# Head sums of a linear-attention trunk as two rounded products, at later places of the plan

## The reference

```python
def gla_out(o, r, norm_w):
    o = o * lax.rsqrt(jnp.mean(o * o, axis=-1, keepdims=True) + EPS) * norm_w.astype(jnp.float32)
    bsz, h, n, dv = o.shape
    o = o.transpose(0, 2, 1, 3).reshape(bsz, n, h * dv)
    return (o * jax.nn.silu(r.astype(jnp.float32))).astype(r.dtype)
```

## Time and profile before

| | |
|---|---|
| median of 3 runs | 1081.17 us (1080.87 to 1081.6) |
| the profiled execution | 1081.7 us |
| its span, first to last instruction | 1079.9 us |
| PE busy | 1055.8 us, 98% |
| DVE busy | 825.2 us, 76% |
| ACT busy | 510.8 us, 47% |
| POOL busy | 307.3 us, 28% |
| mean granted clock of PE | 0.997 |

### The profile page before, as it was taken

How to read it: one execution, slowest core, us unless ns; L and a number is a source line. 1 busy time by engine, 2 the same in 40 slices (tenths; PEclk the granted TensorE clock), 3 DMA queues, 4 the chain that set the end, 5 groups by cost and what they waited for, 6 DMA issues and landing times.

```text
span 1079.9 us, 16429 instructions
## 1 busy us (share of the span) xinstructions
PE 1055.8 (98%) x5576; PEld 852.4 (79%) x5576; DVE 825.2 (76%) x1062; ACT 510.8 (47%) x827; POOL 307.3 (28%) x280
## 2 busy tenths in 40 slices
PE   8999999999999999999999999999999999999996
PEld 5678888777778888887888888888778888888884
DVE  4878868647455986899887787877987777787776
ACT  5666533456525222677766666676422222222234
POOL 1000006486101443012332323233322222222323
PEclk9999999999999999999999999999999999999998
DMA  9633331101013664226866666768745844864604
GB/s 352 247 98 118 117 117 40 40 22 40 21 56 120 253 221 169 78 98 234 316 246 260 227 273 233 257 248 298 296 167 234 350 193 178 329 267 179 254 1 156
DMA packets 66646, 199.82 MB, mean 185 GB/s; under 512 B 5664, under 2 KB 15136, under 8 KB 66592
## 3 DMA queue, kind: packets, MB, share of 16 engines
q1 hardware_dynamic: 66592, 199.11, 49.2%
HBM read 139.32 MB, written 59.77 MB: 184 GB/s over the span
## 4 chain that ended last, share of the span: by engine, by line
PE 49%; DVE 5%; issue 1%; DVEq 0%; ACT 0%
PE main L1453 13%; PE ob L1411 13%; PE sm L1411 10%; PE sm L1453 8%; PE ob L1453 6%; DVE stage L2562 1%; DVE XR L2681 1%; DVE XR L2748 1%; DVE slot L2507 1%; DVE slot L2512 1%; DVE stage_last L2562 0%; DVE t_tmp L2555 0%; DVE hid L2569 0%; DVE t_tmp L2546 0%; DVE t_tmp L2541 0%
## 5 line engine op out<-in xcount | busy, mean ns | idle before, releaser
L958 PE MATMUL main<-a_hi,w_hi 128*128 128x512 f32 x376 | 125.9, 416 | 0.0
L1411 PE MATMUL ob<-h_sum,slot 128*128 128x512 f32 x504 | 121.2, 389 | 2.2 <-DVE hid L2569 2.1
L1882 ACT ACTIVATE slot<-raw 128x512 fp32r<-128x512 f32 x80 | 50.2, 631 | 153.1 <-PE main L1453 58.4
L958 PE MATMUL main<-a_lo,w_hi 128*128 128x512 f32 x376 | 116.5, 391 | 0.0
L958 PE MATMUL main<-a_hi,w_lo 128*128 128x512 f32 x376 | 116.2, 390 | 0.0
L1411 PEld LDWEIGHTS ob<-h_sum,slot 128*128 128x128 f32 x504 | 94.5, 188 | 22.5 <-issue 2.5
L2681 DVE SCALAR_TENSOR_TENSOR XR<-main,small,XR 128x512 f32<-128x512 f32 x112 | 83.3, 748 | 28.8 <-PE main L1453 27.7
L958 PEld LDWEIGHTS main<-a_lo,w_hi 128*128 128x128 f32 x376 | 70.6, 188 | 15.6
L958 PEld LDWEIGHTS main<-a_hi,w_lo 128*128 128x128 f32 x376 | 70.6, 188 | 15.5
L958 PEld LDWEIGHTS main<-a_hi,w_hi 128*128 128x128 f32 x376 | 66.7, 188 | 18.0 <-issue 5.8
L1453 PE MATMUL main<-t_even,slot 128*128 128x512 f32 x336 | 78.1, 389 | 0.0
(11 more groups left out here) (338 smaller groups left out, 2448.3 us busy)
## 6 DMA issues: line engine op xcount, KB each, us to landing
hidden_kept<-stage SPq DMA_DIRECT2D x98, 512.0 KB, 4.3
raw<-wstream SPq DMA_DIRECT2D x60, 512.0 KB, 4.2
t_even<-hidden_kept SPq DMA_DIRECT2D x56, 512.0 KB, 5.4
raw<-wstream SPq DMA_DIRECT2D x16, 1024.0 KB, 5.5
stage<-hidden_kept SPq DMA_DIRECT2D x21, 512.0 KB, 5.1
stage_last<-hidden_kept SPq DMA_DIRECT2D x21, 512.0 KB, 5.9
wmod<-wm SPq DMA_DIRECT2D x8, 1024.0 KB, 10.5
mbuf<-wm SPq DMA_DIRECT2D x16, 512.0 KB, 4.0
```

Source lines behind the costliest of these rows:

```text
L958: ins = pe.matmul(main[:, bank, half * HALF:(half + 1) * HALF], w[:, slot, k, :], x[:, half * HALF:(half + 1) * HALF], start=begin, stop=end)
L1411: ins = pe.matmul(hid_bank(acc, odd), slots1[j][:, w, kp, :], parts[x][:, kp, :], start=PARTS[j][3] and kp == 0 and m == 0, stop=kp == KP ...
L1882: act.activation(slots2[j][:, 0, :, :, :], operand(s, j), ACT.Copy).then_inc(w2_hi, 1)
```

## The change

Each head's squares are split into a rounded part (sqo_hi, made by a copy on ACT) and a low part (sqo_lo, made by a subtraction on DVE in a new job "sl"). Each head sum becomes two rounded products with a rounded matrix of ones (ones_r, made once) that are added up in the bank. The sums move to later places: from 4 and 5 places behind the first O of their head to 6 and 7 (heads 0 and 2) or 8 and 9 (heads 1 and 3). The first group's pooling products move from 10.6 and 10.7 to 10.4 and 10.5, and the decay of head 3's states from 14.1 and 14.2 to 14.4 and 14.5. The new buffers take the places of old ones: sqo_lo overwrites sqo, and sqo_hi lies where rso does.

```diff
-MIX_AT = (9 * 8, 11 * 8 + 6, 13 * 8 + 2, 14 * 8 + 1)
+MIX_AT = (9 * 8, 11 * 8 + 6, 13 * 8 + 2, 14 * 8 + 4)
+SPLIT_AT = (4, 4, 3, 4)
+SUMS_AT = (6, 8, 6, 8)
...
-    put_all(OUT_AT[_h] + 4, 1, ("ns", _h, 0), ("ns", _h, 1))
+    put_all(OUT_AT[_h] + SPLIT_AT[_h], 1, ("sl", _h))
+    put_all(OUT_AT[_h] + SUMS_AT[_h], 1, ("ns", _h, 0), ("ns", _h, 1))
...
-    put(10, 6 + _i, "pl", 0, _i)
+    put(10, 4 + _i, "pl", 0, _i)
...
+        sqo_lo = at("sqo_lo", [P, N], F32R, ZF + 10 * KIB)
+        sqo_hi = at("sqo_hi", [P, N], F32R, ZF + 14 * KIB)
...
             def head_sums(h, i):
                 b = begin_small(("ns", h, i))
-                pe.wait_ge(sqo_made, h + 1)
-                pe.matmul(sm[:, b, :], ones, sqo[:, i * HALF:(i + 1) * HALF], start=True, stop=True).then_inc(small_done, 1)
+                pe.wait_ge(sqo_split, h + 1)
+                cols = slice(i * HALF, (i + 1) * HALF)
+                pe.matmul(sm[:, b, :], ones_r[:, :], sqo_hi[:, cols], start=True, stop=False)
+                pe.matmul(sm[:, b, :], ones_r[:, :], sqo_lo[:, cols], start=False, stop=True).then_inc(small_done, 1)
...
                     act.activation(sqo[:, :], ob[:, :], ACT.Square).then_inc(sqo_made, 1)
+                    act.wait_ge(sqo_made, h + 1)
+                    if h == 0:
+                        act.activation(ones_r[:, :], ones, ACT.Copy)
+                    act.activation(sqo_hi[:, :], sqo[:, :], ACT.Copy).then_inc(sqo_rounded, 1)
...
+            def square_low(h):
+                dve.wait_ge(sqo_rounded, h + 1)
+                tt(sqo_lo[:, :], sqo[:, :], sqo_hi[:, :].bitcast(F32), ALU.subtract).then_inc(sqo_split, 1)
+
...
-            jobs = {"ch": chain_states, "A": scores, "ns": head_sums, "md": mod_product}
+            jobs = {"ch": chain_states, "A": scores, "sl": square_low, "ns": head_sums, "md": mod_product}
```

More of the change, by code:

```diff
@@ L304, in hybrid_trunk @@
         macc = at("macc", [P, N], F32, ZF + 5 * KIB)
-        scaled_state = at("scaled_state", [P, DV], F32, ZF + 9 * KIB + 256)
+        scaled_state = at("scaled_state", [P, DV], F32, ZF + 9 * KIB)
+        ones_r = at("ones_r", [P, P], F32R, ZF + 9 * KIB + 512)
         mbuf_late = at("mbuf_late", [P, 4, N], F32, ZD)
@@ L425, in hybrid_trunk @@
         sqo_made = sem("sqo_made")
+        sqo_rounded = sem("sqo_rounded")
+        sqo_split = sem("sqo_split")
         rso_made = sem("rso_made")
```

## The result

The changed kernel takes 1087.8 us (median of 6 runs, 1086.3 to 1088.62), the kernel before beside it 1081.38 (1079.4 to 1081.75): a ratio of 1.0061, 95% interval 1.0051 to 1.0070. It is 0.6% slower. Forecast were 1086.2 us, 1083.5 to 1088.5, and slower with a chance of 0.85.

The account below looks back on a forecast made before the run. PE, busy 98% of the span, was taken to bound the kernel. The profiled 1081.7 us, plus 3.7 for waits less savings, plus 1.3 for the clock, less 0.5 to the median, gave 1086.2 us; range 1083.5 to 1088.5.

Parts of the forecast that it names:

- Part 1: Head sums on PE: two rounded products take 0.46 us instead of 0.87; eight sums save 3.3 us.
- Part 2: Extra work per head: ACT copy 1.03 us, DVE subtraction 1.23, the latter costing PE nothing; one ACT copy under 0.3.
- Parts 3 and 4: Heads 0 and 1: bank waits leave head 0 only 0.1 us gained, head 1 nothing; head 2's scores 0.6 later.
- Part 5: Head 2's second sum: PE waits 6.1 us for ACT's Ln; head 3's scores start 4.6 us later.
- Part 6: Head 3's sums: 0.82 us gained; everything behind keeps its order, so the summed +3.7 us stays to the end.
- Part 7: Clock falling in the long wait before head 3's scores: costs 1.3 us, the middle of 0 and 2.5.
- Rival 1: At head 3's scores: the wait comes but the clock costs nothing, 1084.9 us; chance 0.25.
- rivals 2 and 3: Scores of head 3: bank freed before needed, 1076.9 us, chance 0.08; wait only 2 to 3 us, 1081.3, chance 0.07.
- rival 4: Head sums: two rounded products cost as much as the fp32 one, saving of 3.3 missing, 1088 us; chance 0.03.

Follow-up runs that it names:

- the last two runs: Twins on one chip, changed kernel with head 1's and 2's sums and the decays re-placed: with the split 1078.41 us, with fp32 products 1080.94 us.
- the filled wait: Changed kernel plus 22 unused rounded products between the two bank waits of head 3's scores: 1084.94 us, ratio 1.0051.
- one place earlier: Changed kernel with both sums of head 2 one place earlier, at 14.6 and 14.7: 1081.75 us, ratio 1.0009.
- places alone: Changed kernel's places without the split: old fp32 head sums, no rounded copy, no subtraction: 1087.72 us, ratio 1.0071.
- decay put back: Changed kernel with only the decay of head 3's states back at 14.1 and 14.2: 1086.4 us, ratio 1.0041.
- the best version: Changed kernel with head 2's sums one place earlier, head 1's behind head 3's updates, decays of heads 2 and 3 later: 1078.22 us, ratio 0.9965.
- without the low part: Changed kernel without the subtraction on DVE, one rounded product for each sum: 1086.95 us, ratio 1.0050.
- the split without the places: Changed kernel with sums, pooling products and decay at their old places, low part at the first sum's place: 1098.93 us, ratio 1.0165.

## Why the prediction was right, and where its sizes were off

**Part 1** held. A sum is two products, 0.22 to 0.23 apart, and the next product follows 0.45 after the first, the price of a pair. The last two runs measured 2.5 for what six or eight of them save.

**Part 2** held for ACT (copy 1.06, ones 0.31 once) but not for DVE at head 0, where I let the subtraction cost nothing. It took 2.16 beside POOL's addition, which it delayed; POOL the sum had left out altogether.

**Parts 3 and 4** held in kind: there were 0.78, 0.84 and 0.34 of waiting for banks, and 11.2 only 0.18 earlier (-2.10 against -1.92) where I had 0.1. Missed was the wait of 1.19 at head 1's outputs for the decay. I stopped following head 0's gain at 11.2 and didn't ask when POOL's chain, and with it the decay, would be ready. So at 13.5 the changed kernel was not 0.6 but 1.92 - 0.39 = 1.5 later, measured from head 0.

**Part 5,** the large term, held nearly to the number: 5.89 instead of 6.1; ACT needed 290.99 - 277.25 = 13.74 from the end of the outputs to the end of the Ln, where my chain had 292.22 - 278.23 = 13.99. Moving head 2's two sums forward by one place took most of it away, and moving the decay behind them the rest. Nothing that left these sums at 14.7 and 15.0 did.

**Part 6** held for head 3 (0.9). That everything behind stays as it was did not hold quite: in the MLP there is a wait for DVE, 2.1 in the profile of before and 3.1 in that of after, and behind it the clock fell in the profile of after alone (0.50 from 512.1 to 515.5). The two together make the last 1.7. Why DVE is later there was not looked into.

**Part 7,** the clock, was the term that was mis-sized: 2.7 behind the wait, where I took 1.3 as the middle of 0 and 2.5. The upper bound was too low, as the clock stayed down 6.8 us, 6.0 of them with PE at work, longer than the 5.1 that it took to fall. I also wrote that no row shows PE at the slow clock. The trace of before does, at its very start: from 3.30 to 9.4 its 128x256 product records begin 0.43 apart and from there on 0.22, some 6 us at half speed or 3 lost, which would have been the better bound. The filled wait shows the term by itself. It varies: behind the shorter waits of three other profiles (one place earlier, places alone, decay put back) it was 1.6. What the Trainium skill says of idle gaps ("TensorE: Matmul & The Clock Gate", section "HAM oscillation — how this bites in real kernels") is borne out at this wait: PE idles, the clock drops, the next work starts at the slow clock; here 0.50 was granted from 290.2 to 297.1. **Rival 1,** no cost of the clock, is refuted by this execution and by the filled wait, **rivals 2 and 3** by the wait, and **rival 4** by the last two runs.

Sum: 5.0 was forecast over the median of before, 6.4 came. In the two profiles, measured from head 0, it is 8.9: the clock term's 1.4, the decay's 0.9 and the MLP's 1.7 were missing, and all three make it slower. That the median came out nearer than this is in part luck: the profile of before lost 0.8 to 1.9 more, ahead of head 0, than any of the eleven later ones, and the clock in the MLP differs from execution to execution. The medians don't divide the difference further.

## What to carry to other kernels

When work on the bounding engine gets cheaper or moves, list for each small job which buffer it takes, who empties that buffer, and what stands ahead of the emptying in that engine's own order; two jobs in one place that share a buffer turn the reader's whole backlog into a wait. A later place is safe against the inputs and may be fatal for the buffers behind it: the same 3.3 us of saved work came out as 6.4 slower at one set of places and as 2.3 and 3.5 faster, in two series of runs, at another. Follow a gain past the first place that takes it back, up to the slowest chain on the other engines. And where a wait in the bounding engine may let its clock fall, price both, the wait and the slow work behind it.

## What the runs showed of the hardware that I had not expected

A short wait can be followed by the slow clock as well. After 1.8 us of waiting the clock fell a microsecond into the new work, and the scores were 5.17 apart instead of 3.57. And it needn't fall after a longer one. The MLP's wait stands in all twelve profiles. It was 3.24 in both of the best version, and the clock stayed at 1.00; it was 3.0 to 3.1 in five others (the changed kernel among them), and the clock fell each time. It was 2.1 in the remaining five: the clock fell in two (decay put back, without the low part) and stayed in three (the kernel before, the split without the places, the wait filled). Each time it was at 0.50 for 3.4 us. Idle time alone, as seen in these rows, doesn't tell whether it falls; in the wait that was filled with work it didn't.

DVE and POOL slowed each other at head 0, by 0.9 us each (2.16 for 1.23 and 2.89 for 2.02). In every profile with the subtraction POOL's addition took 2.89, and in the four without it (the kernel before among them) 2.02 or 2.03; the subtractions of the other heads took 1.21 to 1.23. Yet a weight's low part of the same length, on DVE beside POOL's earlier multiplication, took its usual 1.23. Which pairs of instructions collide was not tried.
